# The Fourier products of a two-block transformer use half the rows, and the layer norm's sums of squares go ahead of them

## What is computed

```python
def _fourier_mix(v, fw):
    b, l, _ = v.shape
    vg = v.reshape(b, l, B_GROUPS, B_GROUP_DIM).astype(jnp.float32)
    f = jnp.fft.fftn(vg, axes=(1, 3), norm='ortho').real.astype(v.dtype)
    return jnp.einsum('blgd,gde->blge', f, fw).reshape(b, l, B_WIDTH)

def _even_mix(h, w_in, a_conv_w, a_conv_b, a_ln_g, a_ln_b, a_pw_w, a_pw_b, b_fw, w_out):
    a_val, a_glu, a_gate, b_val, b_gate = _split(h @ w_in, [A_WIDTH, A_WIDTH, A_WIDTH, B_WIDTH, B_WIDTH])
    u = a_val * jax.nn.sigmoid(a_glu)
    u = jax.nn.silu(_layernorm(_dwconv(u, a_conv_w) + a_conv_b, a_ln_g, a_ln_b))
    y_a = (u @ a_pw_w + a_pw_b) * jax.nn.silu(a_gate)
    y_b = _fourier_mix(b_val, b_fw) * jax.nn.silu(b_gate)
    return jnp.concatenate([y_a, y_b], axis=-1) @ w_out
```

## Time and profile before

| | |
|---|---|
| median of 3 runs | 818.92 us (818.89 to 818.97) |
| profiled execution | 819.54 us |
| its span | 817.5 us |
| TensorE busy | 758.8 us, 93% of the span |
| VectorE busy | 643.6 us, 79% |
| ScalarE busy | 388.6 us, 48% |
| GpSimd busy | 55.2 us, 7% |
| granted TensorE clock, mean | 0.986 of full speed |

### The profile page before, as it was taken

One profiled execution on the slowest core, in us unless ns is written; L12 is line 12 of the kernel. 1 busy time (PEld: TensorE's weight loads), 2 busy tenths in 40 slices (PEclk: granted clock), 3 DMA queues, 4 the chain that ended last, 5 costly groups with the idle time before them and its releaser, 6 DMA issues.

```text
span 817.5 us, 13124 instructions
## 1 busy us (share of the span) xinstructions
PE 758.8 (93%) x5479; PEld 701.5 (86%) x5480; DVE 643.6 (79%) x997; ACT 388.6 (48%) x521; POOL 55.2 (7%) x35
## 2 busy tenths in 40 slices
PE   0399999989899999999998999999989999999996
PEld 0399999979898999999998998887667899899995
DVE  3987777996966799999867769999749965896752
ACT  2354656637355655454546632323363444455742
POOL 0000000000000132222311000000410000000000
PEclk9899999999999999999999999999999999999999
DMA  9999998765643566676646041322103622663101
GB/s 345 417 347 346 352 358 309 264 238 179 249 177 131 188 249 234 231 276 252 250 177 233 26 156 51 104 63 92 53 0 129 268 97 85 232 249 143 61 1 52
DMA packets 26086, 156.58 MB, mean 192 GB/s; under 512 B 2691, under 2 KB 7084, under 8 KB 7852
## 3 DMA queue, kind: packets, MB, share of 16 engines
q1 hardware_dynamic: 21392, 148.91, 49.3%
q10 hardware_dynamic: 4636, 6.85, 2.5%
HBM read 154.68 MB, written 1.06 MB: 191 GB/s over the span
## 4 chain that ended last, share of the span: by engine, by line
PE 58%; DVE 28%; issue 6%; ACT 5%; ACTq 1%; DMA 1%; POOL 1%; DVEq 0%
PE psum L1273 47%; DVE w_lo L806 7%; DVE arena L1039 6%; DVE w_lo L836 5%; DVE att L1039 3%; ACT w_hi L355 2%; PE psum L1561 1%; PE psum L1308 1%; PE psum L1732 1%; DMA raw<-in_w 1%; PE psum L1708 1%; PE psum L1720 1%; POOL arena L315 1%; PE psum L1415 1%; DVE arena L992 1%
## 5 line engine op out<-in xcount | busy, mean ns | idle before, releaser
L1273 PE MATMUL psum<-h_hi,w_hi 128*128 128x256 f32 (+1 forms) x1312 | 398.8, 304 | 15.9 <-DVE h_lo L872 10.1
L1273 PE MATMUL psum<-h_lo,w_hi 128*128 128x256 f32 (+1 forms) x1312 | 393.3, 300 | 0.0
L1273 PE MATMUL psum<-h_hi,w_lo 128*128 128x256 f32 (+1 forms) x1312 | 393.0, 300 | 0.0
L1273 PEld LDWEIGHTS psum<-h_hi,w_hi 128*128 128x128 f32 x1312 | 252.3, 192 | 27.6 <-issue 15.2
L836 DVE TENSOR_TENSOR w_lo<-raw,w_hi 128x2048 fp32r<-128x2048 f32 x93 | 212.7, 2288 | 73.4 <-ACT w_hi L355 72.4
L1273 PEld LDWEIGHTS psum<-h_lo,w_hi 128*128 128x128 f32 x1312 | 252.7, 193 | 7.9 <-issue 0.2
L1273 PEld LDWEIGHTS psum<-h_hi,w_lo 128*128 128x128 f32 x1312 | 252.6, 193 | 7.5
L355 ACT CAST w_hi<-raw 128x2048 fp32r<-128x2048 f32 x93 | 177.0, 1905 | 28.5 <-DMA raw<-in_w 23.6
L806 DVE SCALAR_TENSOR_TENSOR w_lo<-raw,cond 128x1024 fp32r<-128x1024 f32 x88 | 119.4, 1393 | 0.7
L806 DVE SCALAR_TENSOR_TENSOR w_lo<-raw,arena 128x1024 fp32r<-128x1024 f32 x48 | 56.8, 1220 | 1.1 <-DMA raw<-in_w 0.6
L315 POOL TENSOR_TENSOR arena<-arena 128x512 f32<-128x512 f32 x11 | 26.0, 2367 | 390.0 <-ACT arena L569 390.0
(11 more groups left out here) (214 smaller groups left out, 792.3 us busy)
## 6 DMA issues: line engine op xcount, KB each, us to landing
raw<-in_w SPq DMA_DIRECT2D x141, 1024.0 KB, 4.9
xs<-in_xs ACTq DMA_DIRECT2D x2, 1024.0 KB, 13.0
consts<-diff ACTq DMA_DIRECT2D x8, 128.0 KB, 7.0
cond<-in_cond ACTq DMA_DIRECT2D x1, 1024.0 KB, 7.0
out<-xs SPq DMA_DIRECT2D x4, 256.0 KB, 2.4
arena<-in_cond ACTq DMA_DIRECT2D x1, 512.0 KB, 7.0
consts<-in_c ACTq DMA_DIRECT2D x1, 512.0 KB, 3.5
arena<-in_c ACTq DMA_DIRECT2D x1, 448.0 KB, 3.2
```

What stands on the lines that cost most here:

```text
L1273: last = mm(out, w[a], x[b], start=start and n == 0, stop=stop and n == 2, skip_group_check=skip)
```

## The change

The tables of cosine and sine keep their first 128 rows. The symmetry needs the sum and the difference of token n and token 256 - n. GpSimd makes them for each half of the channels: the difference into `b_diff`, the sum in place into `b_val`. `fourier_a` has three matmuls of 128 columns for each s (cosine part of the sums, sine part of the differences, and one with a single weight column for token 128) in place of two of 256. Its result has 256 columns, ScalarE copies 256, and `fourier_b` has four matmuls in place of eight. The order changes too. TensorE makes the sums of squares before `fourier_b(2)`, and `fourier_b(3)` stands between the second and the third column tile of the pointwise product. ScalarE has `fourier_out(2)` behind the table load and `fourier_evac(3)` behind the first Silu. `fourier_out(3)` stays where it was.

```diff
+            for half in range(2):
+                v = b_val[:, 2 * half:2 * half + 2, :].rearrange("p t (s n) -> p t s n", s=2)
+                near, far = v[:, :, :, 1:P], v[:, :, :, T - 1:P:-1]
+                pool.wait_ge(sem("ein_evac"), 5 + half)
+                pool.memset(b_diff[half][:, :, :, 0:1], 0.0).then_inc(sem("b_zeroed"), 1)
+                nc.gpsimd.tensor_tensor(b_diff[half][:, :, :, 1:P], near, far, ALU.subtract).then_inc(sem("b_folded"), 1)
+                pool.wait_ge(sem("b_folded"), 1 + 2 * half)
+                nc.gpsimd.tensor_tensor(near, near, far, ALU.add).then_inc(sem("b_folded"), 1)
...
-                    nc.scalar.copy(four[s], bank[2 * s][:, :]).then_inc(sem("four_ready"), 1)
+                    nc.scalar.copy(four[s], bank[2 * s][:, 0:T]).then_inc(sem("four_ready"), 1)
...
-            fourier_out(2)
             act.wait_ge(sem("ln_sumsq"), 1)
...
             preload(ACT.Silu)
-            fourier_evac(3)
+            fourier_out(2)
...
+                if t == 0:
+                    fourier_evac(3)
...
                 for s in range(2):
-                    for lt in range(2):
-                        last = mm(bank[2 * s][:, lt * T:(lt + 1) * T], b_val[:, g, s * T + lt * P:s * T + (lt + 1) * P],
-                                  fold[:, g, :, :].rearrange("p c n -> p (c n)"), start=True, stop=True)
-                    last.then_inc(sem("four_a"), 1)
+                    out = bank[2 * s]
+                    mm(out[:, 0:P], b_val[:, g, s * T:s * T + P], fold[:, g, 0, :], start=True, stop=True, skip_group_check=True)
+                    mm(out[:, P:T], b_diff[g // 2][:, g % 2, s, :], fold[:, g, 1, :], start=False, stop=False, skip_group_check=True)
+                    mm(out[0:1, P:T], b_val[:, g, s * T + P:s * T + P + 1], fold[:, g, 0, :], start=False, stop=True,
+                       skip_group_check=True).then_inc(sem("four_a"), 1)
...
-                    for q, (part, table) in enumerate(((0, cos_l), (1, sin_l))):
-                        for lt in range(2):
-                            last = mm(bank[1][:, s * T:(s + 1) * T], four[s][:, lt * T + part * P:lt * T + (part + 1) * P],
-                                      table[:, lt, :], start=(q == 0 and lt == 0), stop=(q == 1 and lt == 1))
+                    for q, table in enumerate((cos_half, sin_half)):
+                        last = mm(bank[1][:, s * T:(s + 1) * T], four[s][:, P * q:P * (q + 1)], table, start=(q == 0), stop=(q == 1))
...
-            fourier_b(2)
             pe.wait_ge(sem("ein_evac"), 10)
             for t in range(4):
                 pe.wait_ge(sem("ln_squares"), t + 1)
                 last = mm(wide[:, 3, :], ones, ln_tmp[:, t, :], start=(t == 0), stop=(t == 3))
             last.then_inc(sem("ln_sumsq"), 1)
+            fourier_b(2)
             fourier_a(3)
-            fourier_b(3)
...
             for m in range(4):
+                if m == 2:
+                    fourier_b(3)
```

More of the change, by code:

```diff
@@ L110 @@
 N_C1 = 896
-N_C2 = 1280
+N_C2 = 768
 N_C3 = 896
@@ L191, in ffn_g @@
             return g_hi[:, :, :], g_lo[:, :, :]
-        cos_l = consts[:, 0:512].rearrange("p (l n) -> p l n", n=T)
-        sin_l = consts[:, 512:1024].rearrange("p (l n) -> p l n", n=T)
+        cos_half, sin_half = consts[:, 0:256], consts[:, 256:512]
         dft_d = att[:, 2048:2304]
@@ L206, in build @@
         y_b = b_val
-        four = [att[:, 0:512], att[:, 512:1024]]
+        four = [att[:, 0:256], att[:, 256:512]]
+        b_diff = [a[:, 512:1024].rearrange("p (t s n) -> p t s n", t=2, s=2) for a in (att, consts)]
         diffs = [att[:, 1024 + 2 * UW * n:1024 + 2 * UW * (n + 1)].rearrange("p (s n) -> p s n", s=2) for n in range(2)]
@@ L514, in _ @@
             act.wait_ge(sem("pv_stick"), 4)
-            act.dma_start(consts[:, 0:1024], c2_d[:, 0:1024]).then_inc(sem("c2_loaded"), 16)
-            act.dma_start(dft_d, c2_d[:, 1024:1280]).then_inc(sem("c2_loaded"), 16)
+            act.dma_start(consts[:, 0:512], c2_d[:, 0:512]).then_inc(sem("c2_loaded"), 16)
+            act.dma_start(dft_d, c2_d[:, 512:768]).then_inc(sem("c2_loaded"), 16)
             act.dma_start(fw, fw_d).then_inc(sem("c2_loaded"), 16)
@@ L1546, in fourier_a @@
                     pe.wait_ge(sem("ein_evac"), 6)
+                pe.wait_ge(sem("b_zeroed"), 1 + g // 2)
+                pe.wait_ge(sem("b_folded"), 2 + 2 * (g // 2))
                 for s in range(2):
-                    for lt in range(2):
-                        last = mm(bank[2 * s][:, lt * T:(lt + 1) * T], b_val[:, g, s * T + lt * P:s * T + (lt + 1) * P],
-                                  fold[:, g, :, :].rearrange("p c n -> p (c n)"), start=True, stop=True)
-                    last.then_inc(sem("four_a"), 1)
+                    out = bank[2 * s]
[3 more added lines that the diff above has]
+                       skip_group_check=True).then_inc(sem("four_a"), 1)
             def fourier_b(g):
@@ L1806, in shape_constants @@
     scale = 1.0 / np.sqrt(T * P)
-    cos_l = (np.cos(ang) * scale).reshape(2, P, T).transpose(1, 0, 2).reshape(P, 512)
-    sin_l = (-np.sin(ang) * scale).reshape(2, P, T).transpose(1, 0, 2).reshape(P, 512)
+    cos_half, sin_half = (np.cos(ang) * scale)[0:P], (-np.sin(ang) * scale)[0:P]
+    sin_half[0] = np.where(l % 2 == 0, scale, -scale)
     d = np.arange(P)
@@ L1821, in shape_constants @@
     band = np.concatenate([np.where(j <= i, 0.0, 8 * NEG), np.where(j >= i, 0.0, 8 * NEG)], 1)
-    c2 = np.concatenate([cos_l, sin_l, np.cos(ang), np.sin(ang)], 1).astype(f)
+    c2 = np.concatenate([cos_half, sin_half, np.cos(ang), np.sin(ang)], 1).astype(f)
     c3 = np.concatenate([np.cos(a), np.sin(a) * sign, swap, band], 1).astype(f)
```

## The result

The changed kernel takes 827.14 us (median of 4, 826.94 to 828.83) against 818.9 us for the kernel before: ratio 1.0113, with a 95% interval of 1.0100 to 1.0125. The two medians alone give 1.0101, which is inside that interval. It is slower, by 8.2 us where 6.1 were forecast (9.3 us by the ratio). The profiled execution after is the slowest of the four, 828.83 us with a span of 826.7; before, the span was 817.5.

What follows compares the result with a forecast made beforehand. VectorE's work up to the last tap at 584.63 and the chain behind it were taken to decide. Minus 3.7, plus 3.1, 4.0, 2.2 and 0.5 gave plus 6.1 us on the median 818.92: 825.0 us, range 820.5 to 829.0.

Steps and rivals of the forecast that it cites:

- Direction and range: Whole kernel: slower, 825.0 us, range 820.5 to 829.0; chance of slower by over 0.2% was 0.83.
- the likeliest case: Whole kernel: folds hold the taps and the clock falls; 825.0 us, own range 822.5 to 828.5, chance 0.55.
- The folds: Up to the last tap: GpSimd's four folds block VectorE, 3.6 us; with a possible second gate-product pause, plus 4.0 us.
- The order behind Ln: Behind Ln: on ScalarE, fourier_out(3) waits for fourier_b(3) and delays the split and y_a casts; plus 3.1 us.
- The way from the last tap to Ln: Last tap to Ln: the order with fourier_b(2) off the chain gives minus 3.7 us, TensorE's half clock plus 2.2.
- The clock ahead of the pointwise product: Ahead of the pointwise product: a second TensorE idle time puts part of m=0 and m=1 at 1.2 GHz; plus 0.5 us.
- Folds that cost nothing: Rivals at the taps: folds slip past VectorE; 821.0 us if the clock falls (chance 0.12), 818.3 if it holds (0.14).
- A clock that stays: Rival at TensorE's restart: folds hold the taps, but the clock stays or returns before it matters; 822.3 us, chance 0.13.

Runs made afterwards that it cites:

- Experiment 2: The changed kernel without the four folds on GpSimd, two memsets that read nothing in their place; ratio 1.0068 to the kernel before.
- experiment 3: The changed kernel with fourier_out(3) moved on ScalarE behind the split and the second y_a cast; ratio 1.0090 to the kernel before.
- experiment 1: The changed kernel with 42 matmuls of zeros on TensorE while it waits for the last tap; ratio 1.0083 to the kernel before.
- experiments 7 and 9: Changed kernel, all Fourier groups ahead of the last column sum, gate products behind the last tap: 0.9970; then folds on VectorE, three column sums in TensorE's gaps: 0.9959.
- experiment 6: The kernel before with sums of squares ahead of fourier_b(2) and GpSimd's gate products held until the last tap is done; ratio 0.9955.

## Why the prediction was right, step by step

**Direction and range.** 827.14 us lies in 820.5 to 829.0, in the likeliest case: folds that hold the taps, and a falling clock. That the median came within 2.1 us of the forecast is in part luck. In the profiled executions the stage grew by 10.3 us where 6.1 were added up, and 1.2 of that was hidden by the earlier entry. The three other executions were 1.6 to 1.9 us shorter than the profiled one.

**The folds.** Right in mechanism, 4.9 us of taps for the 4.0 taken. Experiment 2 puts the four folds at 3.8 us (3.6 foreseen). The other 1.1 are the gate products. I gave the second one half a chance. It came, at 578.59, and the first cost 1.0. Wrong was where GpSimd gets its turn. I named the last tap of a tile and the differences behind it. The first pair did that. The second pair and the second gate product went in behind a split, and the first gate product among taps that ran on without a visible pause.

**The order behind Ln.** Right: the first `y_a` cast at 17.85 us where 17.7 was worked out, turns of 2.16 where 2.2 was, the `y_b` subtractions at 25.6 where 25.5 was, plus 0.5 for the clock. That gives 3.2 us for 3.6 foreseen. What the step didn't see is what lies under ScalarE's wait. With the wait gone (experiment 3), TensorE at half clock leaves only 1.0 us of the 2.8.

**The way from the last tap to Ln.** This is the term that was mis-sized, and it is most of the distance. I took minus 3.7 for the order and plus 2.2 for the clock, minus 1.5 together; the profiled execution had plus 2.2, which is 3.7 of the 4.2 us between 6.1 and 10.3. Two parts of it are measured. At full clock Ln comes 7.7 us behind the tap (experiment 1), not 7.0, so the order gives 3.1. In that chain the sums of squares take 3.69 us and 0.14 of issue ahead of them for the 3.45 that I took, the column sum 1.13 for 0.9, and `fourier_a` 1.7 for 1.4, while the latency behind it was taken 0.2 too long. `fourier_a` wins nothing:

```profile
566.78 0.38 PE L1561 MATMUL psum<-consts,arena 128*128 128x128 f32 x2
567.00 0.39 PE L1562 MATMUL psum<-consts,att 128*128 128x128 f32 x2
567.32 0.38 PE L1563 MATMUL psum<-consts,arena 128*1 128x128 f32 x2
567.63 0.49 PE L1561 MATMUL psum<-consts,arena 128*128 128x128 f32 x2
```

From the first matmul of one half to the first of the next it is 0.85 us, four of the old records of 0.213. I had 0.72, from transposes. The clock cost 5.3 us in this execution (13.0 against 7.7) and 2.3 in experiment 3 with the same code, which is my 2.2. Which of these an execution meets was not something to be read from the trace of before.

**The clock ahead of the pointwise product.** m=0 and m=1 end 13.8 us behind Ln, for the 13.3 that I had worked out at full clock: the 0.5 us that was taken. It could have been more. In experiments 1 and 3, with the same instructions on TensorE behind Ln, they end 14.4 and 15.2 us behind it.

**The rivals.** Folds that cost nothing fell by experiment 2. A clock that stays fell by the windows after.

## What to carry to other kernels

Work that is taken off an engine which waits anyway is worth nothing, and its price still counts: here four folds and the gate products beside VectorE's full stage cost 4.9 us. Before moving a matmul group later, look at who waits for it on the other engines' queues; `fourier_out(3)` held a split and four casts that did not need it. Halved products come out ahead of the kernel before where they let whole groups go ahead of a wait that exists (experiments 7 and 9). Even then they only match the full tables with the sums of squares first and GpSimd's gate products behind the last tap (experiment 6), which is a change of a few lines.

## What the runs showed of the hardware

GpSimd and VectorE take turns at products with two SBUF inputs: taps of 0.48 us took 1.37 to 1.50 beside a product of GpSimd. The Trainium skill ("SBUF — State Buffer", section "SBUF: two separate sides") has the loser wait for the winner's whole instruction. The trace agrees for VectorE: 0.9 to 1.0 us a meeting. GpSimd can lose far more than one instruction, 5.04 and 8.26 us for a product of 1.3 us. The product of 3.01 us lost only the rest of one instruction, the split that ran until 526.46. Which boundary lets it in stays open: one request waited through 18 taps, another (572.71) was served at once among taps of the same kind.

A float32 matmul with a single weight column and 128 columns of data took 0.31 us from its start to the next one's, which lies between the two with 128 weight columns beside it (0.22 and 0.32).

The same instructions after a TensorE idle time of 9.6 us ran at 0.50 clock for nearly the whole way to Ln in one execution (Ln at 13.0 us) and only up to the squares' sums in another (9.9). The four executions of the changed kernel fit that roughly: 828.83, 827.28, 827.00 and 826.94 us at a mean granted clock of 0.977, 0.980, 0.979 and 0.982.
